# Adding the experts' gates into a cleared array in DRAM by indirect DMAs, in place of one-hot matmuls per token

## The chip, the cores and the metric

The kernel runs on one core of one Trainium2 chip. The metric is the device time in microseconds (us) of that core for one execution; lower is better. A kernel's figure is the median of several runs; one more execution was recorded by the hardware profiler, and every row below comes from that one. The engines are PE (matmul), DVE (VectorE), ACT (ScalarE), POOL (GpSimd) and SP, which here only issues the DMAs of the weights.

## The reference

Two transformer blocks for 256 tokens of width 2048. The change touches the last layer of the first block, a mixture of 16,384 tiny experts. Each of 8 heads picks 16 experts for a token; each picked expert gives one dot product with a row of `expert_u`, a gelu, a gate (a softmax over the head's 16 scores), and adds that multiple of a row of `expert_v`:

```python
def peer(h, w_q, sub_keys, expert_u, expert_v):
    xt = h.reshape(T, D)
    q = (xt @ w_q).reshape(T, PEER_HEADS, 2, PEER_DQ // 2)
    s = jnp.einsum('thpd,hpnd->thpn', q, sub_keys, preferred_element_type=jnp.float32)
    s_half, i_half = lax.top_k(s, PEER_TOPK)
    cand = (s_half[:, :, 0, :, None] + s_half[:, :, 1, None, :]).reshape(T, PEER_HEADS, PEER_TOPK * PEER_TOPK)
    cand_idx = (i_half[:, :, 0, :, None] * PEER_NKEYS + i_half[:, :, 1, None, :]).reshape(T, PEER_HEADS, PEER_TOPK * PEER_TOPK)
    top_s, pos = lax.top_k(cand, PEER_TOPK)
    idx = jnp.take_along_axis(cand_idx, pos, axis=-1)
    g = jax.nn.softmax(top_s, axis=-1)
    ...
        a = jnp.einsum('cd,ced->ce', xc, expert_u[ic], preferred_element_type=jnp.float32)
        w = (gc * jax.nn.gelu(a)).astype(xc.dtype)
        return jnp.einsum('ce,ced->cd', w, expert_v[ic])
```

## The kernel before

**Dense experts.** The kernel gathers no expert rows. It multiplies all tokens with all of `expert_u` (stage u: 32 column blocks j of 512 experts, 8 weight pieces each), applies gelu, multiplies element by element with a dense array of gates, which is zero where a token did not pick an expert, and multiplies that with all of `expert_v` (stage v: 16 slices of 1024 experts). A weight piece is 128 x 1024 floats, 512 KB. SP loads it into `raw`; ACT rounds it into `whi` (L1512, hi_split), DVE takes the rest into `wlo` (L1760, lo_split), and PE does three products for each tile (L1312). Five pieces may be loaded and three may be split at a time, so DVE stands about two pieces ahead of PE.

**What sets the order.** Every engine walks through the same Python program and issues its own part of it, in that order; an engine that waits holds all that stands behind it. `step()` is called after most pieces (7 times for the 8 pieces of a block j) and moves each generator in `tasks` and the first one in `idle` by one `yield`. That interleaves side work with the matmuls by count of pieces, not by time.

**Stage u.** After each j, `u_post` puts the gelu of the 512 x 256 results into one of two buffers (ACT L1649) and POOL stores it to `scr_a` (L2264, `gelu_store`). The gelu of j waits until the store of j - 2 has landed. Beside it runs the generator `routing()`. Its first 32 steps pick the best 16 half keys. Then, for each of two groups t of 128 tokens, 24 steps add and pick candidates, compute the gates (`gate_norm`) and find each pick's two half indices (`rank_match`, `rank_pick`, `rank_sum`). PE turns indices and gates so that tokens lie along the free axis (`IDT`). From there 64 groups g of four tokens follow, two steps each: `gate_hot` (DVE L2082 and L2084) builds for each token a one-hot row of the first index (`OA`) and two one-hot rows of the second index times the high and low part of the gate (`OBh`, `OBl`), all in `BH`. `gate_mm` multiplies them on PE into a 128 x 128 map of the token's gates, 8 matmuls for each group; `gate_out` (ACT L1502) copies the maps out of PSUM into `stg`, and after every 8 groups POOL stores 2 MB to `scr_g` (L2258, `gate_store`).

**The hand-over.** `fetch(0)` and `fetch(1)` (POOL L2271 and L2272) read 1 MB each of `scr_a` and `scr_g` for the first two slices, after all stores of the gates have landed (`g_written`). `prepare(0)` waits for them on DVE: `expert_gate` (L2094) multiplies, `expert_split` (ACT L1502, DVE L2101) cuts the product into high and low part in `BH` and `BL`. Each slice of stage v then prepares the next one, and that fetches two ahead.

Of the kernel before, what the change touches and what calls it, by code (L numbers as in the profile page):

```python
# [15 lines left out]
def constants():  # L16
# [5 lines left out]
    c[:, 384:512] = p[None, :]  # L22
# [15 lines left out]
def build(nc, D, out):  # L38
# [12 lines left out]
    with ExitStack() as ctx:  # L51
# [30 lines left out]
        ident, causal, upper, iota = C[:, 0:128], C[:, 128:256], C[:, 256:384], C[:, 384:512]  # L82
# [19 lines left out]
        def heads(x, u):  # L102
# [27 lines left out]
        IDT = M[:, 10240:11008].rearrange("p (a t) -> p a t", a=3)  # L130
        OA = BH[:, 0:4, :].rearrange("p (s x) (y n) -> p s (x y) n", s=2, y=2)
        OBh = BH[:, 4:8, :].rearrange("p (s x) (y n) -> p s (x y) n", s=2, y=2)
        OBl = BH[:, 8:12, :].rearrange("p (s x) (y n) -> p s (x y) n", s=2, y=2)
        gh, gl_ = BH[:, 12, :], M[:, 11008:11264]
        stg = [Yf[:, 0:4096].rearrange("p (i t) -> p i t", t=32),
               M[:, 4096:8192].rearrange("p (i t) -> p i t", t=32)]
# [52 lines left out]
        def walk(steps):  # L189
# [319 lines left out]
            nA = norm_T(lambda t: R[:, t, :], 2048, 0, hl(AH), hl(AL), lambda t: Y[:, t, :], x_sq, x_sq, ssp=ssx)  # L509

# [365 lines left out]

            def routing():
# [7 lines left out]
                t_id = []  # L885
                for t in range(2):
# [11 lines left out]
                    go("gate_gap", fresh("DVE", last, t_id))  # L898
# [3 lines left out]
                    go("gate_norm", sm, ri, fresh("DVE", a))  # L902
# [4 lines left out]
                    for q in range(2):  # L907
                        for h in (0, 4):
# [7 lines left out]
                            go("rank_sum", q, hs, fresh("DVE", a, t_id))  # L916
# [6 lines left out]
                    tc = up("ACT", "ids_out")  # L923
                    misc.give(bank, tc)
                    yield
                wa, th = fresh("ACT", tc, q_read), up("ACT", "gate_hi")
                go("gate_split", wa, fresh("DVE", th))
                ready = [up("DVE", "gate_lo"), latest["PE"]]
                ofree, sfree, tb = {}, {}, {}

                def build_hot(g, k):
                    go("gate_hot", g, k, fresh("DVE", ready, ofree.get(g - 2), q_read))
                    tb[g] = up("DVE", "gate_hot")

                held = {}

                def multiply(g):
                    bank, bfree = yield from wait_for(misc)
                    go("gate_mm", g, bank, fresh("PE", tb[g], bfree))
                    ofree[g] = up("PE", "gate_mm")  # L940
                    held[g] = bank

                def keep(g):
                    go("gate_out", g, held[g], fresh("ACT", ofree[g], sfree.get(g // 8 - 2), ready))
                    tev = up("ACT", "gate_out")
                    misc.give(held[g], tev)
                    if g % 8 == 7:
                        c = g // 8
                        go("gate_store", c, fresh("POOL", tev))
                        sfree[c] = landing(f"gate_stored{c % 2}")  # L950
                        g_written.append(sfree[c])
# [358 lines left out]
        def tensor_program(e):  # L1310
# [139 lines left out]
            def gate_mm(g, bank, ready):  # L1450
                i = g % 2
                for mark in ready:
                    e.wait_ge(*mark)
                for k in range(4):
                    o = banks[bank][:, 128 * k:128 * k + 128]
                    mm(o, OBh[:, i, k, :], OA[:, i, k, :], True, False)
                    last = mm(o, OBl[:, i, k, :], OA[:, i, k, :], False, True)
                last.then_inc(sem("gate_mm"), 1)

# [25 lines left out]
            def na_pv(bank, pt, h, ready):  # L1485
                for mark in ready:
                    e.wait_ge(*mark)
                for t in range(2):
# [8 lines left out]
                  "mla_scores": mla_scores, "mla_pv": mla_pv, "sub_scores": sub_scores, "gate_mm": gate_mm,  # L1497
                  "da_scores": da_scores, "da_pv": da_pv, "na_scores": na_scores, "na_pv": na_pv})

        def scalar_program(e):  # L1500
# [126 lines left out]

            def ids_out(t, bank, ready):
                for mark in ready:
                    e.wait_ge(*mark)  # L1630
                act(IDT[:, :, 128 * t:128 * t + 128], banks[bank][:, 0:384].rearrange("p (a t) -> p a t", a=3), ACT.Copy,
                    "ids_out")

            def gate_split(ready, _):
                for mark in ready:
                    e.wait_ge(*mark)
                act(gh, IDT[:, 2, :], ACT.Copy, "gate_hi")

            def gate_out(g, bank, ready):
                for mark in ready:  # L1640
                    e.wait_ge(*mark)
# [79 lines left out]
        def vector_program(e):  # L1721
# [354 lines left out]
            def gate_hot(g, k0, ready):  # L2076
                i = g % 2
                for mark in ready:
                    e.wait_ge(*mark)
# [357 lines left out]
```

## Time and profile before

| | us |
|---|---|
| median of 3 runs | 3496.22 |
| lowest and highest run | 3491.64, 3498.24 |
| the profiled execution, device time | 3490.94 |
| its span in the trace | 3489.1 |
| PE busy in the span | 3357.1 (96%) |
| DVE busy | 2211.4 (63%) |
| ACT busy | 1505.5 (43%) |
| POOL busy | 83.1 (2%) |

The profiled execution's own time is 1.84 us above its span and 5.28 us below the median of the runs. Busy times are those of the hardware's records. A matmul's record covers its way through the array, longer than the distance to the next one, so groups of matmuls are compared by distances between starts. POOL's DMA instructions have a duration, which is the time that POOL is held by issuing one; when the data has landed is another number.

### The profile page before, as it was taken

How to read it: one execution, taken by the hardware profiler on the slowest of the kernel's cores; microseconds unless marked ns; L12 is line 12 of the kernel's file. 1: busy time of each engine (PE TensorE's matmuls, PEld its weight loads, DVE VectorE, ACT ScalarE, POOL GpSimd, SP SyncE). 2: the span in 40 equal slices, each digit the busy share in tenths (PEclk: the TensorE clock that was granted, in tenths of full speed). 3: DMA queues.
4: the chain of work that ended last, by engine and by line, in shares of the span. 5: the costliest groups of instructions: out<-in, count | busy, mean ns of one | idle time of the engine just before them, and what ended most of it. 6: DMA issues, size and time to landing. Idle time of an engine off the chain costs nothing.

```text
span 3489.1 us, 51823 instructions
## 1 busy us (share of the span) xinstructions
PE 3357.1 (96%) x21588; PEld 3060.9 (88%) x21588; DVE 2211.4 (63%) x3610; ACT 1505.5 (43%) x1918; POOL 83.1 (2%) x107
## 2 busy tenths in 40 slices
PE   7878999999999999999999999999999899999998
PEld 5767899999999997888888878989998799999996
DVE  7766547987777766666666665554455655555555
ACT  3335444444444444444444454434444544444443
POOL 2100000000000000000000000000000000000000
PEclk9989999999999999999999999999999999999999
DMA  4312555665666667666666655444555455555554
GB/s 161 122 41 90 170 182 190 202 198 195 230 209 227 206 240 276 240 241 239 240 240 235 196 171 184 151 163 141 177 184 199 158 184 189 188 188 187 187 188 150
DMA packets 175034, 659.39 MB, mean 189 GB/s; under 512 B 19232, under 2 KB 19232, under 8 KB 171216
## 3 DMA queue, kind: packets, MB, share of 16 engines
q1 hardware_dynamic: 160928, 581.96, 50.2%
q0 software_dynamic: 13872, 74.12, 5.9%
q8 instruction: 170, 2.79, 0.3%
q14 instruction: 64, 0.52, 0.0%
HBM read 620.35 MB, written 35.65 MB: 188 GB/s over the span
## 4 chain that ended last, share of the span: by engine, by line
PE 81%; DVE 4%; ACT 1%; DMA 1%; issue 1%; DVEq 0%; POOL 0%; ACTq 0%; POOLq 0%
PE bank L1312 81%; DVE wlo L1760 1%; ACT whi L1512 1%; PE bank L1354 1%; DMA M<-scr_g 0%; ACT M L1502 0%; DMA scr_g<-M 0%; DVE M L2003 0%; DVE TMP L1823 0%; DVE M L2005 0%; DVE M L2009 0%; DVE R L2195 0%; DVE TMP L1824 0%; DVE M L2007 0%; DVE M L2094 0%
## 5 line engine op out<-in xcount | busy, mean ns | idle before, releaser
L1760 DVE TENSOR_TENSOR wlo<-raw,whi 128x1024 fp32r<-128x1024 f32 x1101 | 1352.0, 1231 | 1034.9 <-ACT whi L1512 1031.4
L1512 ACT ACTIVATE whi<-raw 128x1024 fp32r<-128x1024 f32 x1101 | 1161.4, 1059 | 1409.6 <-PE bank L1312 1399.1
L1312 PE MATMUL bank<-AH,whi 128*128 128x256 f32 (+1 forms) x4112 | 1175.0, 286 | 3.9 <-DVE wlo L1760 3.5
L1312 PE MATMUL bank<-AH,wlo 128*128 128x256 f32 (+1 forms) x4112 | 1163.4, 283 | 0.0
L1312 PE MATMUL bank<-AL,whi 128*128 128x256 f32 (+1 forms) x4112 | 1163.2, 283 | 0.0
L1312 PEld LDWEIGHTS bank<-AH,whi 128*128 128x128 f32 (+1 forms) x4112 | 788.3, 192 | 7.2 <-DVE wlo L1760 4.0
L1312 PEld LDWEIGHTS bank<-AL,whi 128*128 128x128 f32 (+1 forms) x4112 | 788.3, 192 | 0.9
L1312 PEld LDWEIGHTS bank<-AH,wlo 128*128 128x128 f32 (+1 forms) x4112 | 787.8, 192 | 0.1
L1312 PE MATMUL bank<-whi,BH 128*128 128x512 f32 (+1 forms) x1608 | 626.3, 389 | 3.3 <-DVE wlo L1760 3.2
L1312 PE MATMUL bank<-wlo,BH 128*128 128x512 f32 (+1 forms) x1608 | 623.5, 388 | 0.0
L1312 PE MATMUL bank<-whi,BL 128*128 128x512 f32 (+1 forms) x1608 | 623.0, 387 | 0.0
L1312 PEld LDWEIGHTS bank<-whi,BH 128*128 128x128 f32 x1608 | 302.7, 188 | 72.6 <-DVE wlo L1760 7.2
L1312 PEld LDWEIGHTS bank<-whi,BL 128*128 128x128 f32 x1608 | 302.7, 188 | 62.1
L1312 PEld LDWEIGHTS bank<-wlo,BH 128*128 128x128 f32 x1608 | 302.8, 188 | 60.5
L1312 PE MATMUL bank<-whi,AH 128*128 128x512 f32 x640 | 256.4, 401 | 6.8 <-DVE wlo L1760 6.6
L1312 PE MATMUL bank<-whi,AL 128*128 128x512 f32 x640 | 251.7, 393 | 0.0
L1312 PE MATMUL bank<-wlo,AH 128*128 128x512 f32 x640 | 251.6, 393 | 0.0
L1312 PEld LDWEIGHTS bank<-whi,AH 128*128 128x128 f32 x640 | 122.1, 191 | 32.5 <-issue 8.0
L1312 PEld LDWEIGHTS bank<-whi,AL 128*128 128x128 f32 x640 | 121.6, 190 | 26.2
L1312 PEld LDWEIGHTS bank<-wlo,AH 128*128 128x128 f32 x640 | 121.9, 190 | 24.3
L1502 ACT ACTIVATE BH<-M 128x512 fp32r<-128x512 f32 (+1 forms) x97 | 60.6, 630 | 151.1 <-DVE M L2094 150.5
L1986 DVE TENSOR_TENSOR R<-R,bank 128x512 f32<-128x512 f32 x136 | 87.3, 683 | 21.8 <-PE bank L1312 21.8
(240 smaller groups left out, 2241.3 us busy)
## 6 DMA issues: line engine op xcount, KB each, us to landing
raw<-in_peer_u SPq DMA_DIRECT2D x256, 512.0 KB, 3.6
raw<-in_peer_v SPq DMA_DIRECT2D x256, 512.0 KB, 4.3
raw<-in_w_in SPq DMA_DIRECT2D x160, 512.0 KB, 3.5
raw<-in_w_up SPq DMA_DIRECT2D x128, 512.0 KB, 3.4
raw<-in_w_down SPq DMA_DIRECT2D x128, 512.0 KB, 3.5
raw<-in_w_out SPq DMA_DIRECT2D x64, 512.0 KB, 4.0
raw<-in_w_in_a SPq DMA_DIRECT2D x32, 512.0 KB, 3.5
raw<-in_peer_w_q SPq DMA_DIRECT2D x32, 512.0 KB, 4.2
```

The costliest lines, as they stand in the source:

```text
L1312: return e.matmul(outp, l, r, start=start, stop=stop)
L1354: last = e.transpose(banks[bank][:, 128 * n:128 * n + 128], s, ident)
L1502: e.activation(o, x, func, **kw).then_inc(sem(name), 1)
L1512: e.activation(whi[:, n % NH, :], raw[:, n % NR, :], ACT.Copy).then_inc(s_hi, 1)
L1760: e.tensor_tensor(wlo[:, n % NH, :], raw[:, n % NR, :], bf(whi[:, n % NH, :]), ALU.subtract).then_inc(s_lo, 1)
L1986: last = e.tensor_tensor(R[:, t, c], R[:, t, c], b[t][:, :], ALU.add)
```

## The change

`routing()` no longer turns the indices, builds one-hot rows, multiplies or copies. For each group t of 128 tokens `expert_ids` (three small DVE instructions) computes for each of the 8 x 16 picks the place 256 * expert + token in `scr_g`, which is now laid out as [16384 experts, 256 tokens]; `gate_norm` leaves the gates in `GT[t]`, tokens along the partitions. A new task `scatter(t)` then issues 128 indirect DMAs from POOL, each of which adds one column of `GT[t]` (128 floats, one per token) to 128 places of `scr_g`, two DMAs per step. The 16 picks of a head are different experts; two heads may pick the same one, so the first DMA of a head waits until the last of the head before has landed. Since the DMAs add, the array has to be zero first: at the start of the kernel POOL clears 256 columns of `M` and writes them to all of `scr_g` by 8 DMAs of 2 MB. `fetch` reads `scr_g` in the new layout. `routing()` waits by `yield` until both scatters are written out in the program, and then goes on to `fetch(0)`.

The core of the diff:

```diff
+            go("gate_blank")
+            t_blank = up("POOL", "gate_blank")
+            for c in range(8):
+                go("gate_clear", c, fresh("POOL", t_blank))
+                t_clear = landing("gate_cleared")
...
+            def scatter(t, ready):
+                landed = t_clear
+                for h in range(8):
+                    for k in range(16 * h, 16 * h + 16):
+                        go("gate_scatter", t, k, fresh("POOL", ready, landed if k % 16 == 0 else None))
+                        mark = landing(f"gate_scattered{t}")
+                        if k % 2:
+                            yield
+                    landed = mark
+                g_written.append(landed)
...
-                    bank, bfree = yield from wait_for(misc)
-                    tk = transposed(idg, bank, a, tg, bfree)
-                    t_id = [tk]
-                    go("ids_out", t, bank, fresh("ACT", tk, everything))
...
-                for g in range(65):
-                    if g < 64:
-                        build_hot(g, 0)
-                    if g > 0:
-                        yield from multiply(g - 1)
-                    yield
-                    if g < 64:
-                        build_hot(g, 2)
-                    if g > 0:
-                        keep(g - 1)
+                    go("expert_ids", t, fresh("DVE", a))
+                    tasks.append(scatter(t, [tg, up("DVE", "expert_ids")]))
+                    yield
+                while len(g_written) < 2:
                     yield
                 bar.append(everyone())
                 fetch(0)
...
+            def expert_ids(t, ready):
...
+                then(e.scalar_tensor_tensor(out=idg[0], in0=idg[0], scalar=128.0, in1=idg[1], op0=ALU.mult, op1=ALU.add))
+                e.wait_ge(s_vec, at[0])
+                then(e.tensor_scalar(idg[0], idg[0], 256.0, token[:, t:t + 1], ALU.mult, ALU.add))
+                e.wait_ge(s_vec, at[0])
+                e.tensor_copy(EID[t], idg[0]).then_inc(sem("expert_ids"), 1)
...
+            def gate_clear(c, ready):
...
+                rows = D["scr_g"].rearrange("(c p r) t -> c p r t", c=8, p=128)
+                e.dma_start(rows[c], blank.unsqueeze(1).to_broadcast([128, 16, 256])).then_inc(sem("gate_cleared"), 16)
+
+            def gate_scatter(t, k, ready):
...
+                e.indirect_dma_start(out=D["scr_g"].rearrange("e (t o) -> (e t) o", o=1),
+                                     out_offset=bass.IndirectOffsetOnAxis(ap=EID[t][:, k:k + 1], axis=0),
+                                     in_=GT[t][:, k:k + 1], in_offset=None, compute_op=ALU.add
+                                     ).then_inc(sem(f"gate_scattered{t}"), 16)
```

What the change moves on POOL, stage u. Before, the gelu stores (L2264) of the first 14 blocks j and of those behind them, with the 2 MB stores of the gates (L2258) between.

```order
L2264 DMA scr_a<-M 128x1024 [waits gelu] x14
L2258 DMA scr_g<-Y 128x4096 [waits gate_out]
L2264 DMA scr_a<-M 128x1024 [waits gelu] x3
L2258 DMA scr_g<-M 128x4096 [waits gate_out]
L2264 DMA scr_a<-M 128x1024 [waits gelu] x2
L2258 DMA scr_g<-Y 128x4096 [waits gate_out]
L2264 DMA scr_a<-M 128x1024 [waits gelu] x2
```

After, from the first nine gelu stores on, with group t = 0 alone: 14 to 16 scatters (L2205) stand between two gelu stores (L2214), and a head's first scatter waits for the one before it.

```order
L2214 DMA scr_a<-M 128x1024 [waits gelu] x9
L2205 DMA scr_g<-M 4194304x1 [waits gate_cleared,expert_ids,gate_norm]
L2205 DMA scr_g<-M 4194304x1 x13
L2214 DMA scr_a<-M 128x1024 [waits gelu]
L2205 DMA scr_g<-M 4194304x1 x2
L2205 DMA scr_g<-M 4194304x1 [waits gate_scattered0]
L2205 DMA scr_g<-M 4194304x1 x11
L2214 DMA scr_a<-M 128x1024 [waits gelu]
L2205 DMA scr_g<-M 4194304x1 x4
L2205 DMA scr_g<-M 4194304x1 [waits gate_scattered0]
```

And a little later, when both groups scatter at once: 24 and more stand between two gelu stores. The counts of these rows to the fetch are 256 scatters and 12 gelu stores.

```order
L2214 DMA scr_a<-M 128x1024 [waits gelu]
L2205 DMA scr_g<-M 4194304x1 x16
L2205 DMA scr_g<-M 4194304x1 [waits gate_scattered0]
L2205 DMA scr_g<-M 4194304x1
L2205 DMA scr_g<-M 4194304x1 [waits gate_scattered1]
L2205 DMA scr_g<-M 4194304x1 x9
L2214 DMA scr_a<-M 128x1024 [waits gelu]
L2205 DMA scr_g<-M 4194304x1 x20
L2205 DMA scr_g<-M 4194304x1 [waits gate_scattered0]
```

On DVE before, at the start of the one-hot rows in stage u and again at the hand-over: about six small instructions beside each piece, and the wait for the fetch close to the end of the stage.

```order
L2068 TENSOR_REDUCE M<-M 128x64 [waits rank_pick]
L1760 TENSOR_TENSOR wlo<-raw,whi 128x1024 [waits hi_split] x2
L2074 TENSOR_TENSOR M<-M,BH 128x256 [waits gate_hi]
L2082 TENSOR_SCALAR BH<-C,M 128x128 [waits piece_used,gate_lo]
L2084 TENSOR_SCALAR BH<-C,M,BH 128x128
L2084 TENSOR_SCALAR BH<-C,M 128x128
...
L2084 TENSOR_SCALAR BH<-C,M 128x128
L1760 TENSOR_TENSOR wlo<-raw,whi 128x1024 [waits hi_split] x8
L2094 TENSOR_TENSOR M<-M 128x256 [waits gate_fetched0,gelu_fetched0]
L2094 TENSOR_TENSOR M<-M 128x256
L2101 TENSOR_TENSOR BL<-M,BH 128x512 [waits expert_hi]
L1760 TENSOR_TENSOR wlo<-raw,whi 128x1024 [waits hi_split]
```

On DVE after, from the end of routing for t = 1: L1705 is the low part of a piece, L2020 to L2024 are `expert_ids`, L2032 is `expert_gate`. The one-hot rows are gone; the wait for the fetch stands 79 pieces behind the last `expert_ids`, in the middle of stage u, with all later pieces behind it.

```order
L2014 TENSOR_REDUCE M<-M 128x64 [waits rank_pick]
L1705 TENSOR_TENSOR wlo<-raw,whi 128x1024 [waits hi_split]
L2020 SCALAR_TENSOR_TENSOR M<-M 128x128 [waits rank_sum]
L2022 TENSOR_SCALAR M<-M,C 128x128 [waits vector_step]
L2024 CAST M<-M 128x128 [waits vector_step]
L1705 TENSOR_TENSOR wlo<-raw,whi 128x1024 [waits hi_split] x79
L2032 TENSOR_TENSOR M<-M 128x256 [waits gate_fetched0,gelu_fetched0]
L2032 TENSOR_TENSOR M<-M 128x256
L2039 TENSOR_TENSOR BL<-M,BH 128x512 [waits expert_hi]
L1705 TENSOR_TENSOR wlo<-raw,whi 128x1024 [waits hi_split]
```

At the start of the kernel POOL now has the clearing (L2194, L2200) between the loads of the inputs and its first subtraction for the bias (L2181).

```order
L2174 DMA ST<-in_table 128x64
L2194 MEMSET M 128x256
L2200 DMA scr_g<-M 2048x1x256 [waits gate_blank]
L2200 DMA scr_g<-M 2048x1x256 x7
L2181 ISA
L2181 TENSOR_TENSOR Y<-POS 128x1024 [waits lo_split,piece_used,hi_split,pos_landed]
```

## Rows read from the trace of the kernel before

**Rows 1.** The page: span, busy time of each engine.

```profile
span 3489.1 us, 51823 instructions
PE 3357.1 (96%) x21588; PEld 3060.9 (88%) x21588; DVE 2211.4 (63%) x3610; ACT 1505.5 (43%) x1918; POOL 83.1 (2%) x107
```

**Rows 2.** Stretches: from:to and length, busy us (instructions) of each engine, clock, DMA share, GB/s.

```profile
0.00:100.00 100.00, 70.50 (x376) 59.04 (x376) 73.96 (x126) 37.26 (x59) 21.75 (x18) 0.98 0.44 151
780.00:1280.00 500.00, 500.00 (x4204) 500.00 (x4203) 375.67 (x917) 213.52 (x258) 14.38 (x27) 1.00 0.63 215
1320.00:1370.00 50.00, 46.70 (x208) 37.01 (x208) 33.33 (x43) 23.40 (x27) 3.41 (x5) 1.00 0.82 283
```

**Rows 3.** PE's waits, 1290 to 1375 us: for whom, us in total, times, longest.

```profile
PE bank L1312 <- DVE wlo L1760: 5.0, 7, 1.8
```

**Rows 4.** Groups by line, 780 to 1320 us: busy us, mean ns, idle before.

```profile
L1312 PE MATMUL bank<-BH 128*128 128x128 f32 x512 | 64.6, 269 | 0.0
L1760 DVE TENSOR_TENSOR wlo<-raw,whi 128x1024 fp32r<-128x1024 f32 x167 | 204.5, 1224 | 139.3 <-ACT whi L1512 139.2
L2084 DVE TENSOR_SCALAR BH<-C,M 128x128 fp32r<-128x128 f32 x256 | 87.5, 342 | 0.0
L2082 DVE TENSOR_SCALAR BH<-C,M 128x128 fp32r<-128x128 f32 x256 | 71.8, 281 | 0.0
```

**Rows 5.** Timeline of PE in stage u around one group of gate matmuls.

```profile
848.84 0.28 PE L1312 MATMUL bank<-AH,wlo 128*128 128x256 f32 x1
848.96 1.01 PE L1312 MATMUL bank<-BH 128*128 128x128 f32 x8
849.80 0.33 PE L1312 MATMUL bank<-AH,whi 128*128 128x256 f32 x1
```

**Rows 6.** Timeline of POOL in stage u: start, duration.

```profile
733.13 0.53 POOL L2264 DMA_DIRECT2D scr_a<-M  x1 [22.83 <-ACT M L1649]
756.17 0.53 POOL L2264 DMA_DIRECT2D scr_a<-M  x1 [22.50 <-ACT M L1649]
...
827.70 0.53 POOL L2264 DMA_DIRECT2D scr_a<-M  x1 [23.73 <-ACT M L1649]
854.31 0.53 POOL L2264 DMA_DIRECT2D scr_a<-M  x1 [26.08 <-ACT M L1649]
...
1301.27 0.54 POOL L2271 DMA_DIRECT2D M<-scr_a  x1 [2.04 <-DMA scr_g<-M]
```

**Rows 7.** POOL's groups over the whole span: busy us, mean ns, idle before.

```profile
L2264 POOL DMA_DIRECT2D scr_a<-M x32 | 17.1, 534 | 895.5 <-ACT M L1649 895.5
L2272 POOL DMA_DIRECT2D M<-scr_g x16 | 14.5, 906 | 1.9 <-issue 1.9
```

**Rows 8.** DMA issues: count, KB each, median us from issue to landing.

```profile
scr_a<-M POOLq DMA_DIRECT2D x32, 512.0 KB, 3.4
scr_g<-M POOLq DMA_DIRECT2D x4, 2048.0 KB, 8.6
```

**Rows 9.** Timeline of DVE: ends of routing for both groups, and the hand-over.

```profile
725.09 1.21 DVE L2068 TENSOR_REDUCE M<-M 128x64 f32<-128x1024 f32 x1
...
808.97 1.23 DVE L1760 TENSOR_TENSOR wlo<-raw,whi 128x1024 fp32r<-128x1024 f32 x1 [0.23 <-ACT whi L1512]
...
1315.57 0.76 DVE L2094 TENSOR_TENSOR M<-M 128x256 f32<-128x256 f32 x2 [4.36 <-DMA M<-scr_g]
```

**Rows 10.** The start: two stretches of 10 us, and POOL's timeline.

```profile
0.00:10.00 10.00, 0.00 (x0) 0.00 (x0) 2.10 (x6) 3.45 (x7) 2.48 (x8) 1.00 0.80 269
10.00:20.00 10.00, 2.79 (x12) 2.42 (x12) 6.39 (x24) 5.67 (x12) 0.00 (x0) 1.00 0.74 293
...
47.72 4.19 POOL L2243 TENSOR_TENSOR Y<-POS 128x1024 int32<-128x1024 int32 x2 [44.19 <-PE bank L1312]
60.73 2.81 POOL L2243 TENSOR_TENSOR Y<-POS 128x1024 int32<-128x1024 int32 x1 [8.81 <-DVE Y L1872]
65.49 1.90 POOL L2243 TENSOR_TENSOR Y<-POS 128x1024 int32<-128x1024 int32 x1 [1.95 <-DVE Y L1872]
```

More of the change, by code:

```diff
@@ L129, in build @@
         idg = [M[:, 9728 + 128 * i:9856 + 128 * i] for i in range(3)]
[L130 to L136, printed above, removed]
+        GT = [M[:, 10240 + 256 * i:10368 + 256 * i] for i in range(2)]
+        EID = [M[:, 10368 + 256 * i:10496 + 256 * i].bitcast(u32) for i in range(2)]
+        blank = M[:, 11904:12160]
         gels = [M[:, 2048 + 1024 * i:3072 + 1024 * i].rearrange("p (k n) -> p k n", k=4) for i in range(2)]
@@ L897, in routing @@
                     sm, ri = stat(8), stat(8)
-                    go("gate_gap", fresh("DVE", last, t_id))
+                    go("gate_gap", fresh("DVE", last))
                     a = up("DVE", "gate_gap")
@@ L901, in routing @@
                     a = up("ACT", "gate_exp")
-                    go("gate_norm", sm, ri, fresh("DVE", a))
+                    go("gate_norm", t, sm, ri, fresh("DVE", a))
                     tg = up("DVE", "gate_norm")
@@ L915, in routing @@
                             yield
-                            go("rank_sum", q, hs, fresh("DVE", a, t_id))
+                            go("rank_sum", q, hs, fresh("DVE", a))
                             a = up("DVE", "rank_sum")
                             yield
-                    bank, bfree = yield from wait_for(misc)
-                    tk = transposed(idg, bank, a, tg, bfree)
-                    t_id = [tk]
-                    go("ids_out", t, bank, fresh("ACT", tk, everything))
-                    tc = up("ACT", "ids_out")
-                    misc.give(bank, tc)
-                    yield
[L926 to L951, printed above, removed]
-                for g in range(65):
-                    if g < 64:
-                        build_hot(g, 0)
-                    if g > 0:
-                        yield from multiply(g - 1)
-                    yield
-                    if g < 64:
-                        build_hot(g, 2)
-                    if g > 0:
-                        keep(g - 1)
+                    go("expert_ids", t, fresh("DVE", a))
+                    tasks.append(scatter(t, [tg, up("DVE", "expert_ids")]))
+                    yield
+                while len(g_written) < 2:
                     yield
@@ L1448, in sub_scores @@
                 last.then_inc(s_used if end else sem("sub_scores"), 1)
[L1450 to L1458, printed above, removed]
             def da_scores(bank, h, t, ready):
@@ L1626, in gate_exp @@
                 act(idg[2], idg[2], ACT.Exp, "gate_exp")
[L1628 to L1641, printed above, removed]
-                act(stg[(g // 8) % 2][:, :, 4 * (g % 8):4 * (g % 8) + 4],
-                    banks[bank][:, :].rearrange("p (t i) -> p i t", t=4), ACT.Copy, "gate_out")
             def gelu(gi, b, ready):
@@ L1715, in scalar_program @@
                   "residual_square": residual_square, "q_split": q_split, "sub_out": sub_out, "gate_exp": gate_exp,
-                  "ids_out": ids_out, "gate_split": gate_split, "gate_out": gate_out, "gelu": gelu,
+                  "gelu": gelu,
                   "expert_split": expert_split, "lam_exp": lam_exp, "cols": cols, "da_out": da_out,
@@ L2291, in gpsimd_program @@
             walk({"load_inputs": load_inputs, "distance": distance, "zero": zero, "reload_x": reload_x,
-                  "gate_store": gate_store, "gelu_store": gelu_store, "fetch": fetch, "load_lam": load_lam,
+                  "gate_blank": gate_blank, "gate_clear": gate_clear, "gate_scatter": gate_scatter,
+                  "gelu_store": gelu_store, "fetch": fetch, "load_lam": load_lam,
                   "na_bias": na_bias, "load_post": load_post})
@@ L2430 @@
         D[n] = nc.dram_tensor("in_" + n, a.shape, mybir.dt.from_np(a.dtype), kind="ExternalInput").ap()
-    D["scr_g"] = nc.dram_tensor("scr_g", (8, 128, 4096), mybir.dt.float32, kind="Internal").ap()
+    D["scr_g"] = nc.dram_tensor("scr_g", (16384, 256), mybir.dt.float32, kind="Internal").ap()
     D["scr_a"] = nc.dram_tensor("scr_a", (16, 128, 2048), mybir.dt.float32, kind="Internal").ap()
```

42 lines of the change are left out of this document (16 added, 26 removed).

## Prediction

> **What bounds the kernel now.** I read the page first. PE is busy for 3357.1 of 3489.1 us; DVE has 63%, ACT 43%, POOL 2% [rows 1]. Then the stretches: in stage u, 780 to 1280 us, PE has no idle time at full clock, while DVE works 376 and POOL 14 of 500 us [rows 2]. So in this stage every matmul that goes away gives back its time, if nothing else becomes late. What the gate matmuls cost is not their mean of 269 ns [rows 4], since records overlap; the distance between starts says it. Eight gate matmuls begin at 848.96, the next matmul at 849.80, and its record is 0.05 us longer than its neighbours' [rows 5]. Eight thus take 0.84 to 0.89 us. The gelu stores say the same over a whole block: 23.04 us from 733.13 to 756.17 without gates, 26.61 us from 827.70 to 854.31 with four groups of them [rows 6], 3.57 us more or 0.89 per group. At the hand-over to stage v PE waits 5.0 us for `wlo` [rows 3], because DVE stands at the products of slice 0, whose fetch lands late [rows 9], and two slices are prepared in a row; PE is busy for 46.70 of 50 us there [rows 2].
>
> **What goes.** 64 groups x 0.89 us = 57.0 us of PE. The one-hot rows (87.5 + 87.5 + 71.8 us of DVE; the second form of L2084 costs as much as the one shown [rows 4]), the copies on ACT and the gates' stores leave engines on which PE does not wait in this stage: nothing. The hand-over's 5.0 us go too, since slice 0 is now prepared some 80 pieces earlier and only slice 1 is left for the border. Sum of the gain: 62.0 us. The three small instructions of `expert_ids`, twice, replace larger ones: nothing. `expert_gate` and the fetch keep their sizes: nothing.
>
> **What comes at the start.** 8 writes of 2 MB. Such a store takes 8.6 us to land [rows 8], so the clearing is up to 69 us of all DMA engines. In the first 100 us these are busy for 44% [rows 2] and thus have 56 us free, but not at once: in the first 20 us, when x and the first pieces come in and everything hangs on them, they are busy for 80% and 74% [rows 10], and POOL issues the clearing right into that. Ends: 0 us if the clearing fills gaps only, 69 us if all of it stands ahead of the weights. I take 10 us: the loads of the first 10 to 20 us, slowed to about two thirds of their pace, and free room later. POOL's subtractions for the bias follow behind it; they are a few us of work at 60 us and after [rows 10], with slack if POOL only issues.
>
> **What comes in stage u: POOL's pace.** This is the term that decides. Let c be the time for which one indirect DMA holds POOL. The scatters of t = 0 can begin behind the gelu store at 733.13 [rows 6], soon after routing for t = 0 ends [rows 9]. There 14 to 16 fall to a block of 23.04 us, so they keep up for any c below about 1.4 us. From the end of routing for t = 1, at about 811 us [rows 9], both groups run, then t = 1 alone: 206 scatters and 10 gelu stores up to the fetch. By when must they be through? DVE waits for the fetch 79 pieces after 811; a piece is 23.04 / 8 = 2.88 us, so at 811 + 228 = 1039 us. From issue (1301.27) to the products (1315.57) the fetch takes 14.3 us now [rows 6, 9]; DVE stands about two pieces ahead of PE, which gives back some 5 us. So the last scatter has to land by about 1030 less the stores' share, say 1027: a window of 216 us. Off it go 10 stores x 0.53 = 5.3 us, seven waits of one head for the head before (twelve in all, ten of them in pairs that share a wait) and the last landing, 8 x 2.9 us = 23 us, where 2.9 is the 3.4 us of the small store to its landing less its issue [rows 7, 8]. It leaves 188 us for 206 scatters: **0.91 us each is free, and each 0.1 us above costs 21 us.** The stall is real time: DVE waits in order, with the low parts of all later pieces behind it, and PE stops two pieces later. Earlier in the stage a late POOL also holds the gelu stores, and the gelu of block j + 2 with them; that is the same lag, not a second one.
>
> No row shows an indirect DMA. Bounds: 0.53 us, a plain DMA on POOL, and 3.4 us, if POOL were held until an issue had landed. The nearest row is the fetch of `scr_g`, whose issue takes 0.91 us because it has 1024 short runs in place of 128 [rows 7]; a scatter has 128 places that are not a pattern but have to be read, each with an addition. I take c = 1.0 us, a tenth above that row: 206 x 0.09 = 18 us.
>
> **The sum.** 3490.9 (the profiled execution) - 57.0 - 5.0 + 10 + 18 = 3456.9 us. The median of the runs is 5.3 us above the profiled execution: **3462 us**.
>
> **Rivals.**
> A, forecast: POOL about keeps up, c below 1.16 us. 3434 us (c at most 0.91, clearing free) to 3489 us. For it: POOL has 486 idle us of 500 [rows 2].
>
> B, slower: POOL's pace becomes the bound. Where c is over 1.16 us, the stall of 206 x (c - 0.91) eats the 62 - 10 = 52 us gained; over 1.20 us the kernel is measurably slower. At 1.5 us the stall is 122 us and the time 3462 + 122 - 18 = 3566 us; at 1.9 us it is 204 us and 3648 us. The place is DVE's wait in L2032, with gelus late before it. For it: the window is full by construction, 28 scatters between two gelu stores while both groups run leave 23.04 / 28 = 0.82 us each, and no row shows an indirect issue. Against it: no POOL issue in the trace takes more than 0.91 us.
>
> C, no change: POOL has to read each column of places from SBUF while DVE reads two operands for `wlo`, 1.22 us in every 2.88 us [rows 4], 42% of the time. If an issue that meets it waits for half of it, c is 0.91 + 0.42 x 0.61 = 1.17 us, the stall 53 us, and the time 3497 us. For it: POOL's equal subtractions take 1.90 us once and 2.81 us another time [rows 10], so something does hold POOL at times. Against it: the plain issues stay at 0.53 us throughout stage u [rows 6]. The Trainium skill has the rule behind this ("SBUF — State Buffer", Who interferes with whom): a DVE instruction with two SBUF inputs contends with a GpSimd instruction that reads SBUF. By the rule C would be the least that is to be expected; by the flat 0.53 us rows it does not reach the issuing of DMAs.
>
> D, far slower: the DMA engines, not POOL, set the pace, since each scatter is 128 separate reads, additions and writes of 4 bytes. If each takes as long as a small store to land, 2.9 us, the stall is 206 x 1.99 = 410 us: 3854 us. It would show as `piece` loads landing late too. Nothing in the trace speaks for or against it.
>
> E, slower from the start: the clearing goes ahead of x and the weights, 69 us in place of 10: 3521 us, all of it before 150 us.
>
> **How the numbers follow.** Chances: A 0.47, B 0.33, C 0.08, D 0.08, E 0.04. A alone gives faster, B, D and E slower. A measurement of this kernel can tell about 0.2%, 7 us. A's own range is 3434 to 3489 us; for 8 in 10 the range has to take in C, E and B up to c = 1.9 us: 3428 to 3650 us, the lower end with a few us more from a lighter DVE. D and the top of B stay outside.
>
> **What would show it.** In the profile of the changed kernel: the distance of gelu stores without scatters stays 23.04 us (else the 57 us are wrong); the issue of a scatter, c, below 0.91 (A at its best), to 1.16 (A, C), above (B); DVE's idle time ahead of L2032, near zero in A and above 50 us in B; ACT's gelu waiting for a store's landing only in B and D; the first matmuls later by up to 10 us than before, by far more in E. The prediction is wrong first of all if c is wrong, and next if the waits between heads last much more than 2.9 us: each further us adds about 8 us.

## The result, and the profile after

| | before | after |
|---|---|---|
| median of the runs, us | 3493.93 | 3713.93 |
| profiled span, us | 3489.1 | 3709.9 |
| PE busy | 3357.1 (96%) | 3319.0 (89%) |
| POOL busy | 83.1 (2%) | 547.1 (15%) |

The changed kernel is slower: 1.0628 times the time of the kernel before, 95% interval 1.0610 to 1.0647. That is 220 us slower, where a time 32 us below this median was forecast (3462 us), and above the range's upper end of 3650 us. PE's busy time fell by 38 us. In the run with 16 scatters (`e2_few_scatters`, below) it fell by 62 us for the same 21070 matmuls; the mean granted clock was 0.987 there and is 0.950 here. PE now stands still for 391 us of the span, before for 132 us.

The page after, its busy times and four lines of its tenths (against [rows 1]):

```profile
span 3709.9 us, 50142 instructions
PE 3319.0 (89%) x21070; PEld 3024.1 (82%) x21070; DVE 2029.6 (55%) x2847; ACT 1471.7 (40%) x1851; POOL 547.1 (15%) x364
...
PE   5978999997353569999999999999999899999998
...
POOL 2100000078888720000000000000000000000000
PEclk8989999998776789999999999999999999999999
```

A slice is 93 us. POOL is at 7 and 8 tenths from about 740 to 1300 us, and PE falls to 3 to 7 tenths one slice later, from about 835 to 1390 us. That POOL is not at 9 there comes from gaps that the page calls "issue". The groups of POOL's instructions (against [rows 7]), with the scatters on top:

```profile
L2205 POOL DMA_INDIRECT scr_g<-M x256 | 458.2, 1790 | 98.2 <-issue 76.1 <-DMA scr_g<-M 22.1
L2200 POOL DMA_DIRECT2D scr_g<-M x8 | 9.1, 1408 | 57.9 <-issue 57.6 <-POOL M L2194 0.3
```

A scatter's record is 1.79 us on the mean, and 0.30 us pass before nearly every one (76.1 us over 250 of them): 2.09 us from one start to the next, where the prediction took 1.0. Who waited for whom, 745 to 1330 us:

```profile
PE bank L1284 <- DVE wlo L1705: 251.6, 11, 45.2
ACT M L1594 <- DMA scr_a<-M: 239.1, 8, 37.3
POOL scr_g L2205 <- DMA scr_g<-M: 22.1, 6, 4.9
DVE M L2032 <- DMA M<-scr_g: 48.4, 1, 48.4
```

PE waits 252 us for low parts. Behind that stand two waits of the same origin: ACT's gelu of block j + 2 waits eight times for the store of block j, which stands in POOL's queue behind some 28 scatters, and at the end DVE waits once for the fetch. The waits of a head for the head before it come to 22 us. The chain of waits for the whole span puts 12% on POOL's L2205, where before POOL had nothing.

POOL's timeline of the fetch, here and in the run with 16 scatters (`e2_few_scatters`, below), in which nothing is late:

```profile
1315.24 0.59 POOL L2221 DMA_DIRECT2D M<-scr_a  x1 [2.10 <-DMA scr_g<-M]
```

```profile
735.99 0.53 POOL L2215 DMA_DIRECT2D scr_a<-M  x1 [22.51 <-ACT M L1595]
...
1027.26 0.57 POOL L2222 DMA_DIRECT2D M<-scr_a  x1 [13.02 <-PE bank L1285]
```

The fetch is issued 288.0 us later. 12.9 us of that stood already at the gelu store ahead of the first scatter (748.89 in place of 735.99 us); the other 275 us are POOL's delay in stage u. DVE's first product comes 284.2 us later (1324.68 in place of 1040.49 us), so some 4 us of POOL's delay cost nothing, and the two spans differ by 283.9 us (3709.9 and 3426.0): start (12.9) and stall (271) are the whole difference.

**The start.** POOL's timeline after (against [rows 10]):

```profile
4.17 7.98 POOL L2200 DMA_DIRECT2D scr_g<-M  x7 [0.30 <-POOL M L2194]
69.78 1.12 POOL L2200 DMA_DIRECT2D scr_g<-M  x1 [57.64 <-issue]
70.93 3.82 POOL L2181 TENSOR_TENSOR Y<-POS 128x1024 int32<-128x1024 int32 x2
```

Seven of the eight writes are issued within 8 us; the eighth is held for 57.6 us, and with it the bias's first subtraction, 70.93 us in place of 47.72. How long the eight writes took to land:

```profile
DMA to landing us min/median/max: 8.4/35.4/58.9
```

The stores of before took 8.6 us [rows 8]. The longest is the seventh: issued at 10.38 us, it lands at 69.3 us, and the eighth begins at 69.78. So the eighth goes out only when the one before it has landed. PE's waits in the first 150 us:

```profile
PE bank L1326 <- DVE Y L1734: 19.6, 1, 19.6
PE bank L1284 <- DVE Y L1817: 13.0, 1, 13.0
```

Before, the same two were 15.2 us and 0.9 us in all: 4.4 us for x coming later, 12.1 us for the bias coming later. Two other rows of this view became shorter (from 7.2 to 5.5 us and from 5.5 to 3.2 us), so PE's idle time in the first 150 us grew by 12.4 us in all, from 34.1 to 46.6. The gelu store ahead of the first scatter stands 15.8 us later than before (748.89 in place of 733.13 [rows 6]) and 12.9 us later than in the run with 16 scatters. So the start costs 12 to 16 us.

### The profile page after: what moved, and what is told of

It is laid out like the page before. It is cut to its first block, busy times and chain, and to the rows that moved or that the text cites. A ratio compares the mean times of both kernels' runs of the same rounds, so it can differ in the third digit from the quotient of the medians.

```text
span 3709.9 us, 50142 instructions
## 1 busy us (share of the span) xinstructions
PE 3319.0 (89%) x21070; PEld 3024.1 (82%) x21070; DVE 2029.6 (55%) x2847; ACT 1471.7 (40%) x1851; POOL 547.1 (15%) x364
## 4 chain that ended last, share of the span: by engine, by line
PE 67%; POOL 12%; issue 3%; DVE 3%; ACT 1%; DMA 1%; DVEq 0%; ACTq 0%; POOLq 0%
PE bank L1284 67%; POOL scr_g L2205 12%; DVE wlo L1705 1%; DMA scr_g<-M 1%; PE bank L1326 1%; ACT whi L1474 1%; ACT M L1464 0%; DMA M<-scr_g 0%; POOL scr_a L2214 0%; DVE TMP L1768 0%; DVE R L2133 0%; DVE TMP L1769 0%; ACT M L1516 0%; DVE AL L1745 0%; DVE ST L1783 0%
## 5 line engine op out<-in xcount | busy, mean ns | idle before, releaser
L1705 DVE TENSOR_TENSOR wlo<-raw,whi 128x1024 fp32r<-128x1024 f32 x1101 | 1349.2, 1229 | 1375.5 <-ACT whi L1474 1371.9
L1284 PEld LDWEIGHTS bank<-AH,whi 128*128 128x128 f32 (+1 forms) x4112 | 797.1, 194 | 258.3 <-DVE wlo L1705 255.2
L1284 PEld LDWEIGHTS bank<-AL,whi 128*128 128x128 f32 (+1 forms) x4112 | 797.2, 194 | 0.9
L1284 PEld LDWEIGHTS bank<-AH,wlo 128*128 128x128 f32 (+1 forms) x4112 | 796.4, 194 | 0.1
L2205 POOL DMA_INDIRECT scr_g<-M x256 | 458.2, 1790 | 98.2 <-issue 76.1
L1594 ACT ACTIVATE M<-bank 128x512 f32<-128x512 f32 x64 | 34.7, 595 | 278.3 <-DMA scr_a<-M 239.1
L1284 PEld LDWEIGHTS bank<-wlo,AH 128*128 128x128 f32 x640 | 122.6, 192 | 24.2
```

The costliest lines, as they stand in the source:

```text
L1284: return e.matmul(outp, l, r, start=start, stop=stop)
L1594: last = e.activation(gels[gi][:, 2 * m:2 * m + 2, :], b[m][:, :].rearrange("p (k n) -> p k n", k=2), ACT.Gelu_apprx_tanh)
L1705: e.tensor_tensor(wlo[:, n % NH, :], raw[:, n % NR, :], bf(whi[:, n % NH, :]), ALU.subtract).then_inc(s_lo, 1)
L2205: e.indirect_dma_start(out=D["scr_g"].rearrange("e (t o) -> (e t) o", o=1), out_offset=bass.IndirectOffsetOnAxis(ap=EID[t][:, k:k + 1], ax ...
```

## The experiments

All of them start from the changed kernel with the clearing moved, so that the start does not blur stage u. The theory: POOL's time for the scatters, beyond the window that the program leaves it, is the loss. Rivals: the DMA engines' small additions; the number of scatters wherever they stand; the cleared array and the fetch in the new layout. The runs with late clearing, with 16 scatters and with half of the tokens were taken four times, the one with one scatter per step twice, the others once. Runs of one kernel lie up to 8 us apart here (3489.99 to 3498.24 us before), so smaller differences are not read.

**The clearing later** (`e1_late_clear`).

```diff
-            go("gate_blank")            (at the start, with its 8 gate_clear)
...
             go("reload_x", fresh("POOL", everything))
             t_x = landing("x_again")
+            go("gate_blank")            (with its 8 gate_clear)
```

> The changed kernel with one difference: the clearing of the gates' array (memset and 8 writes of 2 MB) is issued behind POOL's reload of x, at about 335 us, in place of the start. The trace of the changed kernel shows POOL held from 12 to 70 us ahead of the eighth write and the first gelu store 16 us later than before. Theory (the start's loss is POOL held by the clearing and the loads beside it): 3714 - 16 = 3698 us. Rival (the clearing costs its 69 us of DMA time wherever it stands, since the weights wait for it): no change or worse, 3714 us and above. The loss in stage u is untouched in both.

Measured: 3704.55 us beside 3492.54 us of before, ratio 1.0602 (1.0584 to 1.0620). The median is 9 us below the changed kernel's, less than the 16 us expected, and the two intervals overlap; the sign is likely, the size is not sharp. In its trace the first scatter begins 10 us earlier (739.54 in place of 749.73 us). POOL is held by the eighth write here too (66 us of "issue"), but nobody waits for POOL there, and x is reloaded at 322.07 us in place of 334.83. So what the clearing costs depends on what is queued behind it.

**Sixteen scatters** (`e2_few_scatters`).

```diff
                     for k in range(16 * h, 16 * h + 16):
-                        go("gate_scatter", t, k, fresh("POOL", ready, landed if k % 16 == 0 else None))
-                        mark = landing(f"gate_scattered{t}")
+                        if k == 16 * h:
+                            go("gate_scatter", t, k, fresh("POOL", ready, landed))
+                            mark = landing(f"gate_scattered{t}")
```

> As the kernel with the late clearing, but only the first of the 16 scatters of each head and group is issued, 16 in place of 256; so the gates' array holds one pick in sixteen. Everything else (steps, waits, fetch, layout) stays. Theory (POOL's time for the scatters is the whole loss): before - 57.0 - 5.0 = 3494 - 62 = 3432 us, no stall ahead of the first products. Rival (the new layout of the fetch, the cleared array or the earlier hand-over cost something too): above 3445 us.

Measured: 3430.39 us, ratio 0.9820 (0.9804 to 0.9836), 62.1 us under the kernel before; 62.0 were expected. Gelu stores stand 23.04 us apart again, and DVE does not wait for the fetch. The interval is 57 to 68 us of gain, so the gain side of the prediction is right, and the new layout, the cleared array and the early hand-over cost nothing that these runs can tell. The 16 scatters stand some 18 us apart, and yet none has a record below 1.58 us: the length does not come from scatters queued up behind each other.

**A plain accumulating DMA in place of the indirect one** (`e6_direct`).

```diff
-                e.indirect_dma_start(out=D["scr_g"].rearrange("e (t o) -> (e t) o", o=1),
-                                     out_offset=bass.IndirectOffsetOnAxis(ap=EID[t][:, k:k + 1], axis=0),
-                                     in_=GT[t][:, k:k + 1], in_offset=None, compute_op=ALU.add
-                                     ).then_inc(sem(f"gate_scattered{t}"), 16)
+                rows = D["scr_g"].rearrange("(k p) t -> k p t", p=128)
+                e.dma_start(rows[k, :, 128 * t:128 * t + 1], GT[t][:, k:k + 1], accum_op=ALU.add, allow_slow_non_contiguous=True
+                            ).then_inc(sem(f"gate_scattered{t}"), 16)
```

> As the kernel with the late clearing, but each scatter is a plain accumulating DMA of the same 128 floats to 128 fixed places, 1 KB apart; so the gates land at places that have nothing to do with the picks. Same count, same additions, same bytes, no indices. Theory (indices read by POOL are the cost, not the 4-byte additions on the DMA engines): issue 0.53 to 0.7 us, no stall, 3494 - 62 + 3 = 3435 us. Rival (the DMA engines with 32768 small additions set the pace): issues wait, landings of several us, above 3550 us.

Measured: 3430.44 us beside 3492.42 us, the same as with 16 scatters. One line of its DMA issues:

```profile
scr_g<-M POOLq DMA_DIRECT2D x256, 0.5 KB, 7.0
```

256 of them, each 7.0 us on the way (the median), and PE waits 0.9 us in the whole stage. POOL's first 14, and the stretch 740 to 1030 us of the run with 16 scatters and of this one:

```profile
736.88 12.26 POOL L2206 DMA_DIRECT2D scr_g<-M  x14
```

```profile
740.00:1030.00 290.00, 289.49 (x2409) 289.02 (x2409) 157.53 (x192) 120.87 (x128) 41.78 (x31) 1.00 0.64 205
```

```profile
740.00:1030.00 290.00, 289.51 (x2409) 289.02 (x2409) 157.91 (x192) 120.51 (x128) 227.74 (x267) 1.00 0.93 206
```

The 14 take 12.26 us, 0.88 us each: more than the 0.53 to 0.7 us expected, less than the 0.91 us that are free. Their records overlap (up to 7.0 us long, with starts 0.54 us apart at first), so a record's length is not the time that POOL is held in this run. All 256, with the waits between heads, take 288 us, just within the window. The traffic stays at 205 to 206 GB/s, but the DMA engines' busy share rises from 0.64 to 0.93: at one DMA per 0.88 us the small additions still fit, with little room left. In the stall of the changed kernel, where a scatter comes every 2.09 us, that share is 0.41 to 0.55 in the stretches of 50 us from 880 to 1330 us. So the DMA engines (D in the prediction) do not set the pace there; what costs is POOL's making of an indirect DMA. Whether places drawn by the picks cost the DMA engines more than these fixed ones was not tried by itself.

**Without the addition** (`e5_plain`).

```diff
-                                     in_=GT[t][:, k:k + 1], in_offset=None, compute_op=ALU.add
+                                     in_=GT[t][:, k:k + 1], in_offset=None
```

> As the kernel with the late clearing, but the scatters write their gates and do not add (two heads that pick the same expert for a token would keep one of the two gates). Theory (POOL's 1.55 us is the reading of 128 places and the making of their transfers): issue alone 1.55 us, total near the 3704 us of the late clearing. Rival (the addition is what makes an issue long): clearly below 1.2 us alone, and a kernel below 3550 us.

Measured: 3524.61 us, 180 us faster. This expectation was wrong, and the rival right. The durations (min/median/max) of the scatters in this run, and with the addition in the changed kernel:

```profile
L2205 POOL DMA_INDIRECT scr_g<-M x256: 962/968/2024, 736.5 to 1125.2; - x128
```

```profile
L2205 POOL DMA_INDIRECT scr_g<-M x256: 1541/1552/2599, 749.7 to 1311.6; - x128
```

An indirect DMA of 128 places holds POOL for 0.97 us, and 1.55 us if it adds. The 0.30 us between two are the same in both.

**What lengthens some of them.** In the changed kernel 72 of the 256 begin while DVE is inside the subtraction L1705. They take 2.36 us on the mean, with 0.95 us of the subtraction still to go. The 168 that begin while DVE is idle take 1.55 us, also when a subtraction begins after them. While PE runs unhindered the two lock into step. POOL and DVE from 925 us:

```profile
925.38 2.58 POOL L2205 DMA_INDIRECT scr_g<-M  x1 [0.30 <-issue]
928.27 2.57 POOL L2205 DMA_INDIRECT scr_g<-M  x1 [0.30 <-issue]
```

```profile
925.31 1.23 DVE L1705 TENSOR_TENSOR wlo<-raw,whi 128x1024 fp32r<-128x1024 f32 x1 [1.66 <-ACT whi L1474]
928.19 1.23 DVE L1705 TENSOR_TENSOR wlo<-raw,whi 128x1024 fp32r<-128x1024 f32 x1 [1.65 <-ACT whi L1474]
```

Each scatter begins 0.07 us behind a subtraction's begin, ends 1.42 us behind its end and leaves 0.30 us: 2.88 us, a piece's time, so the next one meets the next subtraction at the same point. Two runs take the second input away from DVE.

```diff
                 e.wait_ge(s_hi, n + 1)
+                if order[n][0] == "peer_u":
+                    e.tensor_scalar(wlo[:, n % NH, :].rearrange("p (a b) -> p a b", a=2),
+                                    raw[:, n % NR, :].rearrange("p (b a) -> p a b", a=2), 0.001, None,
+                                    ALU.mult).then_inc(s_lo, 1)
+                    return
                 e.tensor_tensor(wlo[:, n % NH, :], raw[:, n % NR, :], bf(whi[:, n % NH, :]), ALU.subtract).then_inc(s_lo, 1)
```

> As the kernel with the late clearing, but for the pieces of stage u DVE writes the low part from one input alone (raw times a constant, read with a stride) in place of raw minus whi; so the low parts of that stage are not those of the reference. Same number of elements. Theory (the scatters of 2.58 us are those that meet a DVE instruction with two inputs in SBUF and wait for its end; alone they take 1.55 us): nearly all scatters beside the pieces take 1.55 us, 1.85 us apart; 256 of them plus stores and waits take about 515 us in place of 564, and the kernel is some 45 us faster than the one with the late clearing, about 3650 us. Rival (the long ones come from the DMA engines or from DVE being busy with anything): 2.58 us remains as frequent, 3698 us.

Measured (`e4_one_input`): 3651.42 us, as expected, but not cleanly for the reason expected: DVE's instruction became short too,

```profile
L1706 DVE TENSOR_SCALAR wlo<-raw 128x1024 fp32r<-128x1024 f32 x72 | 50.7, 704 | 335.3 <-ACT whi L1474 335.3
```

and 41 scatters that begin inside one still take 1.77 us, with 0.34 us of it to go. They too end 1.42 us behind the end of DVE's instruction (the median). So this form, with one input, holds POOL until its end just as the subtraction does; it is only shorter. The expectation's "two inputs" is thus not the whole rule. The second run keeps DVE's time (`e9_reduce`):

```diff
+                if order[n][0] == "peer_u":
+                    with nc.allow_low_precision(reason="rounded like the low part"):
+                        e.tensor_reduce(wlo[:, n % NH, :], raw[:, n % NR, :].unsqueeze(2), AX.X, ALU.add).then_inc(s_lo, 1)
+                    return
```

> As the kernel with the late clearing, but for the pieces of stage u DVE writes the low part by a reduction over one element (wlo = raw): one input from SBUF, the same 128 x 1024 elements and about the same 1.2 us of DVE as the subtraction; so the low parts of that stage are not those of the reference. In the run with one strided input DVE's instruction became shorter too (0.70 us), and scatters that began inside one were still held a little, so that run left open what holds them. Theory (POOL is held by the subtraction's two inputs, not by a busy DVE): scatters that begin inside the reduction take 1.55 us as all others; 256 x 1.85 us plus stores and waits, about 515 us, and the kernel near 3650 us. Rival (any DVE instruction of 1.2 us holds POOL for its rest): about 75 scatters of 2.0 to 2.6 us remain, 3704 us.

Measured: 3642.32 us. DVE's instruction and POOL's scatters in it:

```profile
L1707 DVE TENSOR_REDUCE wlo<-raw 128x1024 fp32r<-128x1024 f32 x75 | 90.3, 1218 | 289.6 <-ACT whi L1474 276.1 <-issue 13.5
```

```profile
L2209 POOL DMA_INDIRECT scr_g<-M x256 | 401.5, 1568 | 95.4 <-issue 76.1 <-DMA scr_g<-M 19.2
```

DVE is busy for 1.22 us per piece as ever, 58 scatters begin inside that, and they take 1.55 us. Against the late clearing's 460.3 us of scatters this is 59 us less, and the kernel is 62 us faster (3704.55 to 3642.32 us; this run's kernel before took 3496.72). The hold comes from the form of DVE's instruction, not from a busy DVE. Five scatters of this run begin with over 0.4 us to go in one of routing's own `tensor_tensor` with two inputs (L2006, L2012), and these still take 1.91 to 2.50 us.

**Half of the scatters in the same steps** (`e7_every_second`).

```diff
-                        go("gate_scatter", t, k, fresh("POOL", ready, landed if k % 16 == 0 else None))
-                        mark = landing(f"gate_scattered{t}")
+                        if k % 2 == 0:
+                            go("gate_scatter", t, k, fresh("POOL", ready, landed if k % 16 == 0 else None))
+                            mark = landing(f"gate_scattered{t}")
```

> As the kernel with the late clearing, but only every second scatter is issued (128 in place of 256; half of the picks are missing), spread over the same steps. Window theory (POOL's work counts only beyond the window of 290 us that the program gives it): 128 x 2.2 = 282 us and 14 us of stores, so nearly free: 3435 to 3455 us. Rival (the loss is proportional to the scatters, by whatever they disturb): the 272 us between 3432 and 3704 halved, 3568 us.

Measured: 3478.21 us, 48 us above the run with sixteen. The proportional rival (3568 us) is out, but the expected 3435 to 3455 us were too low:

```profile
L2206 POOL DMA_INDIRECT scr_g<-M x128 | 260.9, 2038 | 59.6 <-issue 35.9 <-DMA scr_g<-M 23.7
```

A scatter is longer here than in the changed kernel, 2.04 us: PE hardly stands still, DVE has a subtraction in every 2.88 us, and 78 of 128 scatters meet one, in place of 72 of 256. 260.9 + 59.6 us and the stores are 339 us from the first to the last, against a window of 290 us (736 to 1027 us in the run with 16 scatters): 49 us, where 48 us are measured. From 16 to 128 scatters the time grows by 48 us, from 128 to 256 by 226 us.

**One scatter per step** (`e8_one_per_step`).

```diff
                         mark = landing(f"gate_scattered{t}")
-                        if k % 2:
-                            yield
+                        yield
```

> As the kernel with the late clearing, all 256 scatters, but each group issues one per step in place of two, so that they are spread over stage u to its end and the fetch comes some 60 steps later. Window theory: from 740 to about 1250 us PE has 510 us of its own work in place of 290; POOL needs 564 us as before if the same share of scatters waits for DVE, up to 256 x 2.88 = 737 us if each piece holds one. Stall 55 to 230 us: 3490 to 3665 us. Rival (what counts is the number of scatters, not where they stand): 3704 us.

Measured: 3550.63 us, ratio 1.0169 (1.0139 to 1.0198), 154 us faster than the same 256 scatters at two per step, though a scatter takes longer (1.97 us on the mean, POOL's time from the first to the last 621 us in place of 564). Only the window grew, to about 510 us: 111 us too much for it, where the run is 120 us above the one with 16 scatters.

**The window in all runs.** Where the program leaves the window of 290 us, POOL's time from the first scatter to the end of the last, less 290 us, can be held against the time above the run with 16 scatters:

| | POOL's time less 290, us | measured above 3430.39, us |
|---|---|---|
| late clearing | 274 | 274 |
| one input | 228 | 221 |
| reduction | 214 | 212 |
| without the addition | 100 | 94 |
| every second | 49 | 48 |

So a loss is POOL's time less the window, within 7 us in these five and 9 us in the run with the longer window, and spreading alone does not make 256 of them fit.

**Half of the tokens by scatter, half by one-hot matmuls** (`e3_half`).

```diff
+                    if t == 0:
+                        go("expert_ids", t, fresh("DVE", a))
+                        tasks.append(scatter(t, [tg, up("DVE", "expert_ids")]))
+                        yield
+                        continue
+                    bank, bfree = yield from wait_for(misc)
+                    tk = transposed(idg, bank, a, tg, bfree)
...
+                for g in range(33):        (one-hot groups of tokens 128 to 255, as before)
...
-                        if k % 2:
-                            yield
+                        yield
```

> A hybrid: the gates of the first 128 tokens are scattered, one DMA per step in place of two, from 128 DMAs in all, into an array of [16384, 128] (8 MB to clear, late); those of the other 128 tokens go through one-hot matmuls as before (32 groups, 4 stores of 2 MB). Theory (a scatter costs PE nothing as long as POOL has over 2.9 us for each; a step is 3.3 us): PE saves 32 x 0.89 = 28.5 us and the 5.0 us of the hand-over: 3494 - 33 = 3461 us, under both kernels. Rival (each scatter costs by itself, by its 128 small additions on the DMA engines beside the weights): half the loss of the changed kernel remains, 3494 - 33 + 130 = about 3590 us.

Measured: 3468.68 us, ratio 0.9930 (0.9913 to 0.9946): 0.7% faster than the kernel before, and faster than the changed one. The stretch 780 to 1280 us (against [rows 2]):

```profile
780.00:1280.00 500.00, 496.36 (x4142) 496.15 (x4142) 311.15 (x577) 209.78 (x242) 259.90 (x148) 1.00 0.73 223
```

POOL works 260 of 500 us here and PE still stands still for 3.6 us only. 24 us of the expected 33 are there. PE's busy time fell from 3357.1 to 3329.8 us, by 27.3 of the 28.5 us expected of the matmuls; the 5.0 us of the hand-over did not come, since PE's waits for `wlo` from 700 to 1600 us are 6.7 us, where the kernel before has 5.5.

The clearing of this run bears on the hold of the start: four writes of 2 MB, each read from the cleared columns in 4096 runs of 512 bytes in place of 2048 of 1 KB, and here the fourth is held.

```profile
320.78 5.03 POOL L2300 DMA_DIRECT2D scr_g<-M  x3 [0.30 <-POOL M L2294]
358.93 1.65 POOL L2300 DMA_DIRECT2D scr_g<-M  x1 [33.12 <-issue]
```

The third lands at 358.5 us. So neither the eighth place nor the bytes make the hold: three writes go out ahead of it here, seven did in the changed kernel. In both, the write that is held brings the runs to 16384; that this count is the limit was not tried by itself.

## Why the prediction was wrong, point by point

**The gain: right.** 62.0 us forecast, 62.1 us measured with sixteen scatters, interval 57 to 68. The distance between starts, not the mean of a record, was the right row.

**The start: half of the mechanism right, size off by 2 to 6 us.** 10 us were taken, 12 to 16 us are seen. The two places were named, x and the bias, but the bias was excused "if POOL only issues". POOL did not only issue: it was held for 57.6 us by the eighth write.

**The term that failed: c.** The term that was mis-sized is the time for which one scatter holds POOL. The step was "the nearest row is the fetch of `scr_g`, whose issue takes 0.91 us", a tenth above which 1.0 us was taken; 2.09 us were measured. The runs give the parts of the true 2.09 us: 0.97 us for 128 indirect places, 0.58 us for the addition, 0.24 us on the mean for waiting on DVE, 0.30 us between two. Nothing in the rows of before priced the first two, and the row taken as nearest was near in one respect only, short runs of a regular pattern. The formula around c held: 206 x (2.09 - 0.91) = 243 us against 271 us measured for the stall. Most of what is missing comes from "they keep up for any c below about 1.4 us": they did not, and when t = 1 joined (DVE's last `expert_ids` at 826.8 us), 32 scatters of t = 0 had been issued where the program had placed 50; 18 x 2.09 = 38 us. With 2.09 us the sum would have read 3490.9 - 62.0 + 12.9 + 243 + 38 = 3723 us, beside 3711.7 us for this profiled execution. The waits between heads and the last landing, taken at 23 us, measure 24.2.

**The rivals.** B was what happened, in place and mechanism: DVE's wait in L2032 (48 us), gelus late before it (239 us of ACT's waits). Its price stopped at c = 1.9 us, and so did the range, though the bound had been given as 3.4 us; between ends as far apart as 0.53 and 3.4 us, the upper part deserved more than the few per cent it got. C's hold is real: estimated at 0.26 us per scatter, measured at 0.24 us. That the two agree is partly luck: 28% of the scatters meet a subtraction in place of 42%, since DVE idles in the stall, and each is held for 0.81 us in place of 0.61. "Against it: the plain issues stay at 0.53 us" was a wrong inference from a DMA without places to one with them: the plain accumulating DMAs begin 0.54 us apart whatever DVE does, the indirect ones are held. That the reading of the places is what meets DVE fits this, but no run separates it from the rest of making an indirect DMA. The Trainium skill's rule ("SBUF — State Buffer", Who interferes with whom), by which a DVE instruction with two SBUF inputs contends with a GpSimd instruction that reads SBUF and a `tensor_reduce` never does, agrees with the traces: 2.36 us inside the subtraction, 1.55 us inside the reduction. D did not happen: see the plain accumulating DMAs and the DMA share in the stall. E happened at about a fifth of its price. A's upper end was mis-summed: c = 1.16 us gives 3495 us by the formula, not 3489; nothing hangs on it.

**The clock.** PE's granted clock falls to 0.57 to 0.80 of full speed in the 50 us stretches from 880 to 1330 us, that is, part of the time at the lower of its two levels (1.2 and 2.4 GHz), after PE has stood idle for up to 45 us. It adds nothing that the sums above would miss: in the stall POOL waits only for landings of its own scatters (22.1 us and 2.1 us) and never for PE, and the span is longer by no more than DVE's first product is late (283.9 and 284.2 us).

## What to carry to other kernels

Before moving work to an engine that is idle, price one unit of it there: an idle share of 97% says nothing where each of 256 units takes 2.09 us and the program leaves 0.91 us for each. Interleaving by count of steps fixes that window in the program's order; an in-order queue turns what does not fit into a stall of everyone whose buffers pass through it, here the gelu stores. Where a unit is cheap as long as it fits, moving only as much as fits (here half) can beat both all and nothing.

## What the runs showed of the hardware that was not expected

- An indirect DMA of 128 places of 4 bytes held POOL for 0.97 us, with an addition 1.55 us, with 0.30 us before the next in either case; a plain accumulating DMA of the same 128 floats took 0.88 us in a row of 14.
- An indirect DMA that began while DVE ran a `tensor_tensor` with both inputs in SBUF waited for its end (2.36 us on the mean, up to 2.60); inside a `tensor_reduce` of the same 1.22 us it did not wait (1.55 us); inside a `tensor_scalar` of 0.70 us with one strided input it waited for the end too (1.77 us, with 0.34 us to go). With periods of 1.85 us and 2.88 us the two engines locked at 2.88 us for as long as PE ran without a stop.
- The eighth write of 2 MB, read in runs of 1 KB and issued from POOL in a row, was held until the seventh had landed, for 57.6 us at the start of the kernel and 66 us at 330 us. With runs of 512 bytes it was the fourth, for 33.1 us. What limit stands behind it was not tried.
- 256 accumulating DMAs of 128 x 4 bytes, one per 0.88 us while they ran, left the traffic at 205 to 206 GB/s but raised the DMA engines' busy share from 0.64 to 0.93; they took 7.0 us to land (the median).
